# Packing small matrix products in a three-layer transformer block: the middle block of a convolution on its own tile, products side by side, and one copy moved

## The reference, cut to what matters

```python
# layer 1: gated linear attention, 4 heads, chunks of C = 64 tokens (nc = 4)
log_a = log_sigmoid(g_low @ gla_gate_up + bias) / 16        # g_low: 16 columns
b = cumsum(chunks(log_a)); b_last = b[..., -1:, :]
q_dec, k_inv, k_dec = qc*exp(b), kc*exp(-b), kc*exp(b_last - b)
attn = where(causal, q_dec @ k_inv.T, 0);  o_intra = attn @ vc
def step(state, (qd, kd, vv, bl)):                           # over the 4 chunks
    o_inter = qd @ state
    state = exp(bl) * state + kd.T @ vv
    return state, o_inter
o = o_intra + o_inter
# layer 1: MoBA attention with 8 heads of 64 over one block of 256 keys (softmax(q k^T / 8 + bias) v)

# layer 2 (even layer)
p = rms_norm(x) @ w_in                                       # a_val, a_gate, ..., q, k, v, ...
u = a_val * sigmoid(a_gate)
u = depthwise_conv_centred(u, conv_w, conv_b)                # 31 taps, 1024 channels
u = silu(group_layer_norm(u, ...))
# mLSTM, forward and backward, 4 heads of 128:
s = (q @ k.T) * exp(D - m_t);  num = s @ v;  den = sum(s)
h = num / max(|den|, exp(-m_t))

# layer 3 (odd layer): attention, 8 heads
pr = softmax(s * scale);  att = pr @ v                       # heads one after the other
```

## Time and profile before

| what | value |
|---|---|
| median of 3 runs | 827.48 us (827.19 to 827.55) |
| the profiled execution's own time | 827.36 us |
| its span, first to last instruction | 825.6 us |
| PE busy | 816.6 us (99%) |
| PE weight loads busy | 696.7 us (84%) |
| DVE busy | 508.8 us (62%) |
| ACT busy | 475.9 us (58%) |
| POOL busy | 41.6 us (5%) |
| chain of work that ended last: share of PE | 98% |

### The profile page before, as it was taken

The page is one execution under the profiler, slowest core; times in us unless marked ns, Lnnn a source line. Parts: engine busy times, 40 slices in busy tenths (PEclk is TensorE's granted clock), DMA queues, the critical chain, the costliest instruction groups (busy, mean ns, idle before and its releaser), DMA issues.

```text
span 825.6 us, 11462 instructions
## 1 busy us (share of the span) xinstructions
PE 816.6 (99%) x4398; PEld 696.7 (84%) x4398; DVE 508.8 (62%) x761; ACT 475.9 (58%) x755; POOL 41.6 (5%) x74
## 2 busy tenths in 40 slices
PE   9999999999999999999999999999999999999997
PEld 7888987888889999888788777788888898898986
DVE  5767762656566666635355676957674567658553
ACT  6558656554356555534546658338864578656642
POOL 2000000000000000510100102000000010000000
PEclk9999999999999999999999999999999999999999
DMA  7773453655466565777557567535465556376121
GB/s 262 240 246 86 146 153 103 204 177 181 152 205 195 182 181 178 192 213 236 171 196 233 161 182 216 174 106 178 131 235 171 168 170 205 104 205 210 44 81 73
DMA packets 84709, 143.38 MB, mean 174 GB/s; under 512 B 9381, under 2 KB 22888, under 8 KB 84528
## 3 DMA queue, kind: packets, MB, share of 16 engines
q1 hardware_dynamic: 80720, 134.37, 52.0%
q0 software_dynamic: 3872, 8.28, 3.7%
q10 hardware_dynamic: 64, 0.02, 0.0%
HBM read 139.44 MB, written 1.07 MB: 170 GB/s over the span
## 4 chain that ended last, share of the span: by engine, by line
PE 98%; DVE 1%; ACT 0%; issue 0%; DVEq 0%; POOL 0%; POOLq 0%; ACTq 0%
PE acc L1736 24%; PE acc L1737 24%; PE acc L1738 24%; PE acc L1792 4%; PE acc L1791 4%; PE acc L1789 4%; PE aux L1825 2%; PE aux L2127 1%; PE aux L2243 1%; PE aux L2067 1%; PE aux L2058 1%; PE acc L1767 1%; PE acc L1766 1%; PE acc L1763 1%; PE acc L1814 1%; PE aux L1979 0%
## 5 line engine op out<-in xcount | busy, mean ns | idle before, releaser
L422 DVE TENSOR_TENSOR wlo<-raw,whi 128x1024 fp32r<-128x1024 f32 (+4 forms) x258 | 303.4, 1199 | 187.9 <-ACT whi L602 186.1
L602 ACT ACTIVATE whi<-raw 128x1024 fp32r<-128x1024 f32 (+4 forms) x258 | 263.5, 1041 | 199.6 <-PE acc L1738 120.8
L1736 PE MATMUL acc<-whi,a_hi 128*128 128x512 f32 (+4 forms) x592 | 226.3, 382 | 0.7 <-issue 0.4
L1738 PE MATMUL acc<-whi,a_lo 128*128 128x512 f32 (+4 forms) x592 | 222.1, 375 | 0.0
L1737 PE MATMUL acc<-wlo,a_hi 128*128 128x512 f32 (+4 forms) x592 | 221.8, 375 | 0.0
L1736 PEld LDWEIGHTS acc<-whi,a_hi 128*128 128x128 f32 x592 | 111.3, 188 | 23.1 <-issue 3.7
L1738 PEld LDWEIGHTS acc<-whi,a_lo 128*128 128x128 f32 x592 | 111.3, 188 | 19.8
L1737 PEld LDWEIGHTS acc<-wlo,a_hi 128*128 128x128 f32 x592 | 111.4, 188 | 19.3 <-issue 0.7
L1736 PE MATMUL acc<-whi,b_hi 128*128 128x512 f32 x214 | 84.1, 393 | 0.0
L1738 PE MATMUL acc<-whi,b_lo 128*128 128x512 f32 x214 | 83.4, 390 | 0.0
L1737 PE MATMUL acc<-wlo,b_hi 128*128 128x512 f32 x214 | 83.3, 389 | 0.0
(11 more groups left out here) (375 smaller groups left out, 906.6 us busy)
## 6 DMA issues: line engine op xcount, KB each, us to landing
raw<-in_even_w_in SPq DMA_DIRECT2D x54, 512.0 KB, 4.4
raw<-in_w_in SPq DMA_DIRECT2D x49, 512.0 KB, 4.4
raw<-in_w_up SPq DMA_DIRECT2D x32, 512.0 KB, 4.5
raw<-in_w_down SPq DMA_DIRECT2D x32, 512.0 KB, 4.4
raw<-in_even_w_out SPq DMA_DIRECT2D x16, 512.0 KB, 4.4
raw<-in_odd_w_in SPq DMA_DIRECT2D x16, 512.0 KB, 4.7
raw<-in_odd_w_out SPq DMA_DIRECT2D x12, 512.0 KB, 4.7
raw<-in_w_branch_gla SPq DMA_DIRECT2D x8, 512.0 KB, 3.4
```

Of the source, the lines that this page charges most:

```text
L422: return e.tensor_tensor(w_view(wlo[u % SPLIT], u), w_view(raw[u % RAW], u), w_view(whi[u % SPLIT], u).bitcast(F32), ALU.subtract)
L602: act.activation(w_view(whi[u % SPLIT], u), w_view(raw[u % RAW], u), ACT.Copy).then_inc(sem("hi_done"), 1)
L1736: pe.matmul(acc_of(c, t), ah[:, ts], hi[:, k], start=first, stop=False)
L1738: ins = pe.matmul(acc_of(c, t), al[:, ts], hi[:, k], start=False, stop=last)
```

## The change

1. **Convolution.** The middle block gets a tile of its own, `AVM`: ACT copies 64 rows of tile 0 and 64 rows of tile 1 into it (`middle_rows`), so `transformed` is three products in the order 0, 2, 1, one per spectrum. In `convolved` blocks 0 and 2 are multiplied whole and the middle block into 64 columns of the array for each output tile. `mcol` stands right behind `transformed(0)`.
2. **Part-row products side by side.** `logits`, the gate product (16 rows at row 0 and 16 at row 32, for which `glT` and `gup` are laid out twice), the states of chunks 0 and 1, and the two spectra of the filter are issued in turn for two parts of the array.
3. **Readouts** stand behind all eight products L1979, those of chunks 1 and 2 in turn, then those of chunk 3.
4. **q and k of the mLSTM** are made by `product_turned` and copied to `EQT` by one ACT step per bank (`channels_out`); the 16 transposes and their copies are gone. The scale 1/rms of q goes to the step that multiplies the decay weights (with k's), and is divided out of the clamp `mcol`.
5. **The tail.** The copy `turned(5)` stands ahead of `exponentials(7)`.
6. On DVE, `mcol` and `gate_values(1)` move ahead, `conv_rows(0)` back; on ACT the weights' pump for `eq` starts its four steps between other work than before.

The diff, cut to its core:

```diff
+BLOCK_ORDER = (0, 2, 1)
...
-        AUX += [("kv", j, i) for j in range(3) for i in range(2)]
+        KV = [(0, 0), (1, 0), (0, 1), (1, 1), (2, 0), (2, 1)]
+        AUX += [("kv", j, i) for j, i in KV]
...
-        glT = sb("glT", [16, TOK], c=c1)
-        gup = sb("gup", [16, 512], c=c1)
+        glT = sb("glT", [64, TOK], c=c1)
+        gup = sb("gup", [48, 512], c=c1)
...
-            pool.dma_start(gup[:, :], A["gla_gate_up"][0]).then_inc(sem("gup_in"), 16)
+            for a in range(2):
+                cs = slice(256 * a, 256 * a + 256)
+                pool.dma_start(gup[32 * a:32 * a + 16, cs], A["gla_gate_up"][0][:, cs]).then_inc(sem("gup_in"), 16)
...
+                def middle_rows(n):
+                    cs = slice(512 * n, 512 * n + 512)
+                    if n == 1:
+                        aux_wait(act, ("fx", 0, 1))
+                    for t, own, other in ((0, slice(0, 64), slice(64, P)), (1, slice(64, P), slice(0, 64))):
+                        act.wait_ge(sem("u_gated"), 2 * n + t + 1)
+                        act.activation(block_rows(1, n)[own], AV[other, t, cs], ACT.Copy).then_inc(sem("u_middle"), 1)
+
+                middle_rows(0)
                 for t in range(NT):
                     copy_out("ea1", AV[:, t, 512:1024], t, scale=rms(2, t))
+                def channels_out(c, w):
+                    for b in range(2):
+                        acc_wait(act, c, b)
+                        acc_free(act.activation(EQT[:, w, 2 * b:2 * b + 2], acc_of(c, b).rearrange("p (k t) -> p k t", k=2),
+                                                ACT.Copy, scale=(1.0, 128.0 ** -0.5)[w]), c)
...
-                for h in range(8):
+                for h in range(7):
                     exponentials(h)
                     if h >= 2:
                         turned(h - 2)
+                turned(5)
+                exponentials(7)
                 turned(6)
                 turned(7)
...
-                        ins = dve.tensor_tensor(DW[:, h, d, o:o + n], DW[:, h, d, o:o + n],
-                                                halves(key)[:, st, a:a + n], ALU.mult)
+                        ins = dve.scalar_tensor_tensor(out=DW[:, h, d, o:o + n], in0=halves(key)[:, st, a:a + n],
+                                                       scalar=rms(2, st), in1=DW[:, h, d, o:o + n],
+                                                       op0=ALU.mult, op1=ALU.mult)
...
-                        for t, j in FROM[i]:
-                            ins = pe.matmul(b[:, :], FT[:, j, 1::2], AV[:, t, 512 * n:512 * n + 512],
-                                            start=j != 2, stop=j != 1)
...
+                        give(pe.matmul(dst[:, :], FT[:, b, 1::2], block_rows(b, n), start=True, stop=True), ("fx", n, b))
...
+                        pe.matmul(dst[t][:, :], FI[:, 3 * t], spectrum(2 * t, 0), start=True, stop=False,
+                                  skip_group_check=True)
+                    ins = [pe.matmul(dst[t][c:c + 64, :], FI[:, 1 + t, c:c + 64], spectrum(1, 0), start=False, stop=True,
+                                     skip_group_check=True) for t, c in ((0, 64), (1, 0))]
...
                 transformed(0)
-                product("eb1")
-                product("eq", 0, 1)
-                pe.wait_ge(sem("fi_in"), 128)
-                convolved(0)
                 pe.wait_ge(sem("m_rows"), 1)
                 b = take(("mcol",))
...
-                product("eq", 1, 4)
+                product("eb1")
+                product_turned("eq", 0, 2)
+                pe.wait_ge(sem("fi_in"), 128)
+                convolved(0)
+                product_turned("eq", 2, 4)
                 transformed(1)
-                product("ek")
...
-                turn_heads(0, "eq")
+                product_turned("ek")
                 product("ev0")
-                turn_heads(1, "ek")
                 convolved(1)
```

More of the change, by code:

```diff
@@ L547, in swap_halves @@
                 def swap_halves(n):
-                    for b in range(3):
+                    for b in BLOCK_ORDER:
                         aux_done(pool, ("fx", n, b))
@@ L687, in _ @@
             aux_wait(act, ("glT",))
-            aux_free(act.activation(glT[:, :], bank(("glT",))[0:16, 0:TOK], ACT.Copy), ("glT",))
+            aux_free(act.activation(glT[:, :], bank(("glT",))[0:64, 0:TOK], ACT.Copy), ("glT",))
             for t, PX in enumerate((P0, P1)):
@@ L881, in _ @@
                     pump("eq", h + 1)
-                for t in range(NT):
-                    copy_out("eq", EQK[:, 0, t], t, scale=rms(2, t))
+                    if h == 0:
+                        middle_rows(1)
+                channels_out("eq", 0)
                 spectra_out(1)
                 pump("ek")
-                for t in range(NT):
-                    copy_out("ek", EQK[:, 1, t], t, scale=rms(2, t))
-                def turned_heads(w):
-                    for j in range(2):
-                        aux_wait(act, ("eqT", w, j))
-                        aux_free(act.activation(EQT[:, w, 2 * j:2 * j + 2], halves(("eqT", w, j)), ACT.Copy,
-                                                scale=(1.0, 128.0 ** -0.5)[w]), ("eqT", w, j))
+                channels_out("ek", 1)
                 def group_rstd(i):
@@ L1474, in _ @@
                 aux_free(dve.tensor_copy(flat(mcol[:, 1]), bank(("mcol",))[:, 16:32]), ("mcol",))
+                pump("eb1", 1)
+                filtered(0)
+                pump("eb1", 2)
+                gate_values(1)
                 pump("eb1")
-                gate_values(1)
+                conv_rows(0)
                 group_stats(0)
@@ L1495, in _ @@
                 dve.wait_ge(sem("clamp"), 1)
+                chain(dve.reciprocal(rinv[:, :], stat[:, 4:6]))
+                for t in range(NT):
+                    ins = dve.tensor_scalar(mcol[:, 1, :, t], mcol[:, 1, :, t], rinv[:, t:t + 1], None, ALU.mult)
+                chain(ins)
                 for h in range(4):
@@ L1960, in _, with state @@
                 aux_done(pe, ("kdt", t))
-            for j in range(3):
+            def state(b, j, h):
                 rows = slice(64 * (j % 2), 64 * (j % 2) + 64)
-                for i in range(2):
-                    b = take(("kv", j, i))
-                    for h in (2 * i, 2 * i + 1):
-                        ins = pe.matmul(b[:, TOK * (h % 2):TOK * (h % 2) + TOK], KDT[rows, j // 2, h],
-                                        GV[rows, j // 2, 256 * h:256 * h + 256], start=True, stop=True)
-                    give(ins, ("kv", j, i))
+                return pe.matmul(b[:, TOK * (h % 2):TOK * (h % 2) + TOK], KDT[rows, j // 2, h],
+                                 GV[rows, j // 2, 256 * h:256 * h + 256], start=True, stop=True)
+            for i in range(2):
+                b0, b1 = take(("kv", 0, i)), take(("kv", 1, i))
+                for h in (2 * i, 2 * i + 1):
+                    ins0, ins1 = state(b0, 0, h), state(b1, 1, h)
+                give(ins0, ("kv", 0, i))
+                give(ins1, ("kv", 1, i))
+            for i in range(2):
+                b = take(("kv", 2, i))
+                for h in (2 * i, 2 * i + 1):
+                    ins = state(b, 2, h)
+                give(ins, ("kv", 2, i))
             product("go1")
@@ L2024, in _ @@
             if STAGES >= 2:
-                pe.wait_ge(sem("wcv_in"), 32)
+                pe.wait_ge(sem("wcv_in"), 64)
+                dst = [take(("ws", n)) for n in range(2)]
+                ins = [pe.matmul(dst[n][:, :], FW[n][:, 1::2], wcv_in[n], start=True, stop=True) for n in range(2)]
                 for n in range(2):
-                    b = take(("ws", n))
-                    give(pe.matmul(b[:, :], FW[:, 1::2], wcv_in[:, 512 * n:512 * n + 512], start=True, stop=True),
-                         ("ws", n))
-                    product("dn1", 7 + n, 8 + n)
+                    give(ins[n], ("ws", n))
+                product("dn1", 7, 9)
             product("dn1", 9, 15)
```

179 lines of the change are left out of this document (90 added, 89 removed).

## The result

| what | before | after |
|---|---|---|
| median | 827.39 us (6 runs, 826.86 to 828.92) | 820.12 us (6 runs, 819.91 to 820.97) |
| the profiled execution's own time | 827.36 us | 819.95 us |
| its span | 825.6 us | 818.2 us |

The account below looks back on a forecast made before the run. The prediction took PE, busy 99% of the span at full clock, to bound the kernel, so work off its list comes off the time. Its terms summed to -7.0 us, 827.4 to 820.4, with 8 in 10 within 819.0 to 822.8.

Parts of the forecast that it names:

- Gate product, filter's spectra: Small-row products on PE run as pairs side by side: -0.86 us for the gate, -1.26 us for the spectra.
- Logits, states: Part-row products of the linear attention, whose halves already overlapped: logits 0, states -0.1 us.
- Readouts: Readouts on PE behind all whole products: -1.0 us, all from fewer switches to part-array products, nothing from the new pairs.
- Transform and back transform: Convolution on PE: three products for four, twice, -1.7 us; back transforms with a middle pair, twice -0.5, -1.0 us.
- q and k: mLSTM products on PE: 16 transposes gone, -1.75 us; turned chunks dearer, +1.4 us with first records; net -0.35 us.
- The order around the filter: PE reaches eq's second unit as DVE, behind the filter, finishes its low part, both at 484.0: +0.1 us.
- B: PE runs into its feeders between 467 and 541; half to all of 3 us comes back, 822 to 823.4; chance 0.15.
- C: Filter's swaps land far too late, PE stands 8.7 us at eq's second unit, slower than before; chance 0.02.
- Tail: Head 5's copy on ACT put ahead of the last exponentials, so PE goes on at 780.58 instead of 781.35: -0.8 us.
- Total: Sum of all terms over the whole kernel: -7.0 us, from 827.4 to 820.4 us.

Follow-up runs that it names:

- experiment 2: Kernel after, with all four gate products in the same 16 rows of the array and both filter products in the same 31 rows: 822.12 us.
- experiment 3: Kernel after, with gate products in four parts of 32 rows at once and the filter's spectra cut into four such products: 819.39 us.
- experiment 10: Kernel after, with logits and states of the linear attention issued in the order of the kernel before, bank after bank: 819.78 us.
- experiment 7: Kernel after, with the readouts of chunk 1 alone and then chunks 2 and 3 in turn: 820.02 us.
- experiment 1: Kernel after, with the middle block of both back transforms multiplied into all 128 columns instead of a pair of 64: 821.21 us.
- experiment 4: Kernel after, with q and k of the mLSTM made by plain products and turned by 16 transposes on PE again: 820.97 us.
- experiment 6: Kernel after, with ACT's copy for head 5 behind the exponentials of head 7 again, as before the change: 820.85 us.
- experiment 9: Kernel after, with 16 already satisfied waits added near the start of DVE's list, nothing else: 819.85 us.
- experiment 5: Kernel after, with six small POOL memsets ahead of the first swap of the filter's half 0, all six swaps issued 2.86 us later: 821.39 us.
- experiment 8: Kernel after, with the low part of eq's second weight unit made by DVE ahead of the filter instead of behind it: 820.31 us.
- experiment 12: Kernel after, with four parts of 32 rows at once for gate product and filter's spectra, and eq's second low part ahead of the filter: 818.93 us.

## Why the prediction was right

The forecast of 820.4 lay 0.3 over the median, and its reading of the kernel held: PE's list alone sets the time, and the sum of what is taken off it is the gain. By its own steps:

- **Gate product, filter's spectra**: right to 0.05, and shown by experiment 2 to be parts of the array working side by side. The four parts of experiment 3 show where the cover ends: PE's next 0.4 there goes to a wait for ACT.
- **Logits, states**: taken as 0 and -0.1, measured 0 and +0.09 (experiment 10). The count of steps in the busier half was the right floor; what it left out is that chunk 2's products now come some 1 us sooner behind those of chunk 0, whose banks they take. Their first records stand 0.29 to 0.32 apart instead of 0.22, which fits a short wait for these banks, though the trace names none.
- **Readouts**: right, and for the reason given (experiment 7).
- **Transform and back transform**: right. The pair's overlap, of which the prediction had only the readouts, with a shorter stream, to go by, held for 512 columns (experiment 1).
- **q and k**: the mis-sized term. Forecast -0.35. The transposes' 1.74 was right; the turned chunks were put at +1.4 and cost 0.59 and 0.53, since the first records that I added for each aren't there: -0.62. Undoing it costs still more, 0.85 (experiment 4), because 0.2 of eq's price lies on time in which PE would wait for the low part anyway, which I had not seen.
- **The order around the filter**: the place was right (PE and the low part meet within tenths), and the size depends on when the swaps land: nothing in experiments 2, 6, 7 and 10, 0.3 in the kernel after, 0.8 in experiment 9. So the +0.1 was a fair middle, and its exact value luck. "Each us later is a us on PE", on which rivals B and C were priced, failed: half of the delay came through (experiment 5). C would thus have needed a larger delay than the text gives. Its 16.1 us was no measure of a swap either: that row is the load of `FT` from memory, while the six swaps of this half took 5.8 to 7.9 us in the kernel before.
- **Tail**: -0.88 at the place itself, against the -0.8 forecast (experiment 6), but +0.28 some us earlier that no step of the prediction had: it goes when DVE's list is 16 instructions longer (experiment 9).
- **Total**: -6.91 against -7.0 from first to last product. The closeness owes something to terms that missed in opposite directions: q and k 0.3 better and 0.15 between the numerators and layer 3, which lies within the scatter of that stretch; the wait in eq 0.2, states with readouts 0.13 and the tail 0.2 worse. The medians differ by 7.3; the 0.4 beyond these pieces is in none of them, and the scatter of the start is large enough to cover it.

## What to carry to other kernels

With one engine at 99%, price each edit by distances between its records at either side, switches between whole-array and part-array products included, and count steps, not products: products in different parts of the array share a step, and only the visit's two ends cost. When a chain gets shorter by tenths, look up who feeds it next, because the feeder's slack may be used up at once, as at 93 us here. Anything queued behind a wait for a transfer inherits its scatter; move what is ready ahead of it, which costs nothing while the engine idles.

## What the runs showed of the hardware that I had not expected

**A start that differs from run to run.** In the 14 profiles (before, after and the 12 experiments) the first product begins at 7.49 to 8.16 us, and the logits, reached by the same work in all of them, at 61.45 to 62.21. The first product hangs on the first weight load and on PE's idle transposes; in experiments 6, 8 and 9 PE then waits again near 11 us for a load of the input, which makes the way to the logits 0.3 to 0.7 longer. The chain after, then the chain before:

```profile
1.31 3.59 DMA raw<-in_w_in
...
7.49 0.47 PE acc L1761
```

```profile
6.28 2.01 PE acc L1814 x10
```

Those ten transposes take 0.21 each before and, in the kernel after, 0.11. PE goes from the one pace to the other at 4.9 us in experiments 1 and 3, at 6.0 after and in experiment 2, and at about 8 before and in experiment 4, although PE is busy in the same way from 1.7 us on in all of them. The granted clock is printed as 1.00 in the rows at either pace, here of the kernel after (window, busy us and counts of PE, PEld, DVE, ACT, POOL, clock, DMA):

```profile
5.00:6.00 1.00, 1.00 (x6) 1.00 (x5) 0.33 (x1) 0.99 (x3) 1.00 (x3) 1.00 1.06 393
6.00:7.00 1.00, 1.00 (x12) 1.00 (x10) 0.89 (x3) 1.00 (x4) 0.16 (x1) 1.00 1.06 351
```

But that 1.00 is no reading at the slower pace. In each of the 14 traces the records of the granted clock begin only where the pace changes, at the full 2.4 GHz level: at 8.04 us before, 5.97 after, 4.91 and 4.89 in experiments 1 and 3, 8.00 in experiment 4. Ahead of that there is no record, and the column shows 1.00. Half the pace fits the lower level of 1.2 GHz, which no record here states. So in the first microseconds PE's pace is to be read from the distances between its records, and a single pair of profiles can't tell a change of half a microsecond there.

**Where an instruction lies in a list.** The same DVE instruction begins 0.35 earlier or later after the same event, by how many instructions precede it: behind 1.47 us of idle in experiments 3, 9 and 12, whose lists are longer, and behind 1.82 to 1.98 in after and the nine others. What happens in DVE at that point no record shows, and it stays open.

**Late transfers that land sooner.** The swaps of 128 KB take 7.2 us beside the weight loads and 5.1 when issued 2.9 us later, by the medians of four. The single ones of the half take 6.0 to 8.1 and 3.3 to 6.7.
